# A two-layer diffusion trunk with experts: the head of the program, the norm ahead of the router and the first expert chunk in another order

## The chip, the cores and the metric

The kernel runs on one core of one Trainium2 chip. The metric is the device time of one execution in microseconds (us), lower is better; several executions are taken and their median is compared. A time below is counted from the start of the profiled span.

## The reference

Two layers work on 256 latent tokens `x` and 256 context tokens `ctx`, each 1024 wide, in float32. Each layer turns a conditioning vector into six modulation rows (shift, scale, gate, twice), for latent tokens from `c` and for context tokens from `c_ctx`. Every sub-layer is `h = x * (1 + scale) + shift; x <- LayerNorm(alpha * x + gate * sublayer(h))`. Cut to what matters:

```python
sc, scc = silu(c), silu(c_ctx)
for l in range(2):
    mod_x = sc @ w_mod[l] + b_mod[l]          # 6 rows of 1024, mod_c alike from scc
    shx1, scx1, gx1, shx2, scx2, gx2 = split(mod_x, 6)
    hx, hc = x * (1 + scx1) + shx1, ctx * (1 + scc1) + shc1
    if l == 0: yx, yc = _mixer_ab(...)        # projection, windowed + neighbourhood attention, output projection
    else:      yx, yc = _mixer_c(...)         # differential attention, latent queries only are needed
    x = _layernorm(DN_ALPHA * x + gx1 * yx, ln_g[l, 0], ln_b[l, 0])
    if l == 0:                                # dense SwiGLU on both streams, norms of ctx and x
        ...
    else:
        h = x * (1 + scx2) + shx2
        logits = h @ w_router                 # 8 experts, top 2 per token, softmax of the two
        f = sum over experts of gate[:, e] * (silu(h @ w_up_g[e]) * (h @ w_up_u[e])) @ w_down[e]
        x = _layernorm(DN_ALPHA * x + gx2 * f, ln_g[l, 1], ln_b[l, 1])
```

## The kernel before

One function, `trunk()`, writes each engine's program by hand, and engines wait for each other on semaphores only. What stands earlier in an engine's program runs earlier: no scheduler reorders it. SP issues the DMAs of all weights, in chunks of 1 MB (128 partitions x 2048 float32), into a ring `RAW` of four slots; the experts' chunks go into a ring of eight (`RAWA`, `RAWB`). A slot is loaded again when its chunk has been used.

**Precision.** Each float32 product is three matmuls (`mm3`, L762 to L764). The operands are a high part (rounded to fp32r) and a low part (the rest): ScalarE (ACT) writes the high part of a weight chunk to `WH` (L1455), VectorE (DVE) the low part to `WL` (L1881). `WH` and `WL` have two slots. The activations' parts are `HH` and `HL` (L1955, L1956); for the experts' weights they are `BH` (L1753) and `RAWAL`/`RAWBL` (L2407).

**The head.** The first eight chunks are half blocks of the modulation's weights, m0 to m7 (L662 to L665). A block is 512 of the 6 x 1024 columns, and a half block covers half the contraction. `mod_half` (L784) makes eight matmuls or four per half, ACT copies the block's rows to SBUF (`mod_row_out`, L1465), `mod_columns` (L775) turns the rows into columns, and DVE adds the bias into `MODC` (L1909): blocks 0 and 1 are the shift of sub-layer 1, blocks 2 and 3 its scale. Then come the projection's weight chunks w0, w1, ... . `h_phase(0)` transposes the tokens `X` on TensorE (PE, L815), ACT applies scale and shift on the way out of PSUM into `F` (L1481), DVE splits `F`. `project(0)` makes tiles of 128 output columns for all 512 tokens, each from eight k-steps of `mm3` (24 matmuls); w0 and w1 hold two tiles each, the first four are here called t0 to t3. The tokens are loaded on POOL's queue. POOL also builds the neighbourhood attention's bias table: rows to DRAM after all eight half blocks are used (L727), from there 16 DMAs into `BIAS` (L735), and DVE adds a mask (L1923) ahead of attention.

**Router.** After layer 1's output projection `residual(2, 1)` (L2142 to L2146) adds the gated result to `X` for the second half of the columns of token blocks 2 and 3 (the latent ones, 128 tokens each), and `norm(2)` makes the layer norm: the statistics of both blocks, one root on ACT, ACT's scaling of `X` (L1643), then on DVE a multiply by the gain and an addition of the bias from `LNR` (L2184, L2185). `h_phase(3)` transposes and modulates as above, `router()` (L1144) makes the logits, DVE and PE work out a table `TAB` of which expert takes which tokens. `experts()` gathers tokens with matmuls (`SEL`): 96 columns for the small slots, 256 for the "big" expert (L1177, L1184), copies them to `FS` and `FE` (L1735, L1741), splits `FE` into `HE` and `LE`, and starts on the experts' chunks. SP reads the experts' numbers from `TAB` into registers and issues the first eight chunks. The fourth chunk is the first one of the big expert: its parts are made after the gathered tokens' ones.

## Time and profile before

| what | us |
| --- | --- |
| median of 3 runs | 1898.12 |
| lowest and highest of them | 1897.44, 1901.23 |
| the profiled execution's own time | 1892.98 |
| its span | 1890.8 |
| PE busy in the span (93%) | 1755.0 |
| DVE busy (41%) | 782.6 |
| ACT busy (35%) | 665.5 |

The span is what the trace covers of the profiled execution; 2.2 us of its time lie around it. The trace's rows are compared with one another inside that execution, which ran 5.1 us below the median. "Busy" sums the instructions of an engine. In a timeline row, "[2.75 <-DMA ...]" says that the engine sat idle for 2.75 us before the row and what ended that. A row "x8" is eight instructions in a row and their time together.

### The profile page before, as it was taken

The numbers are of one execution on the slowest core, as the hardware profiler recorded it, in microseconds if no ns is written. First come the engines' busy times: TensorE is split into PE (matmuls) and PEld (weight loads), VectorE is DVE, ScalarE is ACT, GpSimd is POOL, SyncE is SP. The second block draws the span as 40 slices with busy tenths as digits, with TensorE's granted clock in tenths as the row PEclk, the third lists the DMA queues.
The fourth block names the chain that finished last, engine by engine and source line by source line (L and its number), as shares of the span: only waits on it lengthen the run. The fifth ranks groups of instructions, "written<-read, shape, count | busy, mean of one in ns | idle before, by whom it ended". The sixth has DMA issues, their size and how long they took to land.

```text
span 1890.8 us, 24131 instructions
## 1 busy us (share of the span) xinstructions
PE 1755.0 (93%) x9428; PEld 1216.8 (64%) x9428; DVE 782.6 (41%) x1220; ACT 665.5 (35%) x961; POOL 28.7 (2%) x52
## 2 busy tenths in 40 slices
PE   6999999899999998999768999999899999999997
PEld 3885557688888776976556556655555566565553
DVE  2334553623323255644653443333441433433344
ACT  3224554423222234324634333333334333333241
POOL 2200000000000000000000000000000000000000
PEclk9998999899999999999888999999999999999999
DMA  9734752232322544321009999999989999999986
GB/s 342 162 110 169 259 174 71 67 108 90 117 95 90 202 176 167 112 89 45 5 27 385 421 416 421 421 421 385 421 354 386 385 415 421 420 421 399 413 351 258
DMA packets 111471, 481.81 MB, mean 255 GB/s; under 512 B 8154, under 2 KB 46216, under 8 KB 62208
## 3 DMA queue, kind: packets, MB, share of 16 engines
q1 hardware_dynamic: 108192, 470.57, 63.8%
q0 software_dynamic: 3168, 9.71, 2.1%
q8 instruction: 76, 1.25, 0.3%
q14 instruction: 35, 0.29, 0.0%
HBM read 477.38 MB, written 2.87 MB: 254 GB/s over the span
## 4 chain that ended last, share of the span: by engine, by line
PE 71%; DVE 11%; DMA 8%; ACT 6%; issue 3%; SPq 0%; DVEq 0%; ACTq 0%
PE PS L762 18%; PE PS L764 17%; PE PS L763 17%; DMA RAWB<-in_w_exp_up 5%; PE PS L1254 4%; PE PS L1327 3%; PE PS L784 2%; ACT BH L1753 2%; DVE RAWAL L2407 2%; PE PS L944 1%; PE PS L1202 1%; ACT S L1509 1%; PE PS L954 1%; DMA RAW<-in_w_mod 1%; ACT S L1548 1%
## 5 line engine op out<-in xcount | busy, mean ns | idle before, releaser
L1881 DVE TENSOR_TENSOR WL<-RAW,WH 128x2048 fp32r<-128x2048 f32 (+1 forms) x63 | 142.1, 2256 | 316.1 <-ACT WH L1455 316.0
L762 PE MATMUL PS<-HH,WH 128*128 128x512 f32 (+1 forms) x584 | 225.0, 385 | 5.7 <-DVE HL L1940 4.6
L763 PE MATMUL PS<-HL,WH 128*128 128x512 f32 (+1 forms) x584 | 222.2, 380 | 0.0
L764 PE MATMUL PS<-HH,WL 128*128 128x512 f32 (+1 forms) x584 | 222.1, 380 | 0.0
L1455 ACT ACTIVATE WH<-RAW 128x2048 fp32r<-128x2048 f32 (+1 forms) x63 | 118.8, 1887 | 259.6 <-PE PS L764 228.6
L762 PE MATMUL PS<-BH,HE 128*128 128x512 f32 x448 | 182.2, 407 | 22.4 <-DVE RAWAL L2407 17.0
L2407 DVE TENSOR_TENSOR RAWBL<-RAWB,BH 128x2048 fp32r<-128x2048 f32 x42 | 96.3, 2292 | 211.0 <-ACT BH L1753 211.0
L764 PE MATMUL PS<-BH,LE 128*128 128x512 f32 x448 | 176.5, 394 | 0.0
L1753 ACT ACTIVATE BH<-RAWB 128x2048 fp32r<-128x2048 f32 x42 | 80.4, 1914 | 231.8 <-DMA RAWB<-in_w_exp_up 138.5
L2407 DVE TENSOR_TENSOR RAWAL<-RAWA,BH 128x2048 fp32r<-128x2048 f32 x42 | 96.1, 2289 | 144.8 <-ACT BH L1753 144.8
L762 PEld LDWEIGHTS PS<-BH,HE 128*128 128x128 f32 x448 | 84.7, 189 | 87.2 <-issue 33.9
L1753 ACT ACTIVATE BH<-RAWA 128x2048 fp32r<-128x2048 f32 x42 | 80.4, 1915 | 161.2 <-DMA RAWA<-in_w_exp_up 90.9
L762 PEld LDWEIGHTS PS<-HH,WH 128*128 128x128 f32 x584 | 111.5, 191 | 29.7 <-issue 5.4
L764 PEld LDWEIGHTS PS<-HH,WL 128*128 128x128 f32 x584 | 111.4, 191 | 20.7
L763 PEld LDWEIGHTS PS<-HL,WH 128*128 128x128 f32 x584 | 111.6, 191 | 20.0
L762 PE MATMUL PS<-BH,TH 128*128 128x512 f32 x224 | 93.8, 419 | 16.4 <-DVE TL L2425 16.4
L764 PEld LDWEIGHTS PS<-BH,LE 128*128 128x128 f32 x448 | 85.0, 190 | 18.7
L764 PE MATMUL PS<-BH,TL 128*128 128x512 f32 x224 | 90.3, 403 | 0.0
L763 PE MATMUL PS<-RAWAL,HE 128*128 128x512 f32 x224 | 88.8, 396 | 0.0
L763 PE MATMUL PS<-RAWBL,HE 128*128 128x512 f32 x224 | 87.8, 392 | 0.0
L762 PE MATMUL PS<-WH,HH 128*128 128x512 f32 (+1 forms) x224 | 84.4, 377 | 0.0
L763 PE MATMUL PS<-WL,HH 128*128 128x512 f32 (+1 forms) x224 | 84.0, 375 | 0.0
(313 smaller groups left out, 2723.9 us busy)
## 6 DMA issues: line engine op xcount, KB each, us to landing
RAWA<-in_w_exp_up SPq DMA_DIRECT2D x112, 1024.0 KB, 10.2
RAWB<-in_w_exp_up SPq DMA_DIRECT2D x112, 1024.0 KB, 9.8
...
```

What stands on the lines that cost most here:

```text
L762: mm(ps, ah, bh, start=start, stop=False)
L763: mm(ps, ah, bl, start=False, stop=False)
L764: return mm(ps, al, bh, start=False, stop=stop)
L784: last = mm(PS[k * LANE:(k + 1) * LANE, bank, :], ST[:, kh * 4 + k, :], w[:, k, :], start=(kh == 0), stop=(kh == 1))
L944: mm(PS[:, u % 2, 0:nk], QT[hp, qt, b * P:(b + 1) * P], KTT[hp, kt, 0:nk], start=True, stop=True).then_inc(s_sc, 1)
L954: last = nc.tensor.transpose(PS[:, 2 + n % 2, kt * P:(kt + 1) * P], S[:, i % 2, j, kt * P:(kt + 1) * P], ident)
L1254: last = mm(PS[k * LANE:(k + 1) * LANE, 4 + n % 2, :], FS[:, kh * 4 + k, j * LANE:(j + 1) * LANE], w[:, k, :], start=(kh == 0), stop=(kh = ...
L1327: last = mm(PS[k * LANE:(k + 1) * LANE, 4 + j, :], GS[:, j, st * 4 + k, :], w[:, k, :], start=(st == 0), stop=(st == NST - 1))
L1455: fn(WH[:, c % 2, 0:width(c)], raw("weight", c)[:, 0:width(c)], ACT.Copy).then_inc(s_hi, 1)
L1753: fn(BH[:, a % 2, :], expert_raw(big_at[a]), ACT.Copy).then_inc(s_bhi, 1)
L1881: v.tensor_tensor(WL[:, c % 2, 0:n], raw("weight", c)[:, 0:n], WH[:, c % 2, 0:n].bitcast(F32), ALU.subtract).then_inc(s_lo, 1)
L2407: v.tensor_tensor(expert_low(big_at[a]), expert_raw(big_at[a]), BH[:, a % 2, :].bitcast(F32), ALU.subtract).then_inc(s_blo, 1)
```

## The change

**Head.** SP loads the tokens first, then m0, m1, m2, w0, m3, w1, m4 to m7; w0 and w1 get a buffer of their own (`RAWF`). The half blocks are dealt out so that m0 to m3 give the shift and scale of the first half of the contraction (`mod_block`). PE transposes the tokens before and between the first half blocks, ACT copies them plainly to `F`, and once the modulation is there `F` is modulated in place (two of four rows of chunks by DVE, two by ACT). Then `first_half` makes k-steps 0 to 3 of t0 to t3 into four PSUM banks while m4 to m7 come in, and `project(0)` makes k-steps 4 to 7 of them. ACT's exponential for attention 1's lambda moves from the head to the start of attention 0.

**Router.** The residual and the norm go block by block. PE transposes the normalised tokens without gain and bias; these are folded into the modulation (`MODF`) beforehand. Of `F`, ACT makes rows 0 to 3 and DVE rows 4 to 7. Gain and bias are applied to `X` by POOL, beside the router, and `experts()` waits for that before it gathers. SP reads one expert's number, not all four and the number of items, ahead of its first DMA.

**First big chunk.** Its high part stands on ACT ahead of the copies of `FE`, its low part on DVE ahead of `LE`; the `FE` copies are shared between ACT and DVE.

PE at the start of the program, before: after the transposes of constants come the half blocks m0 to m3 and the columns of block 0 (`RAW` holds the half blocks, `ST` the conditioning vectors).

```order
L768 MATMUL PS<-CN,VRN 128x48
L784 MATMUL PS<-RAW,ST 32x512 [waits raw_landed0,silu_c_pad_zeroed,silu_c_ready]
L784 MATMUL PS<-RAW,ST 32x512 x3
L784 MATMUL PS<-RAW,ST 32x512 [waits raw_landed1]
L784 MATMUL PS<-RAW,ST 32x512 [waits raw_landed2]
L784 MATMUL PS<-RAW,ST 32x512 [waits raw_landed3]
L775 MATMUL PS<-CN,ROWS_AT 128x2 [waits mod_row_copied]
```

PE after the change, from the fourth half block (m3) to the third k-step of t0; L792 to L794 are `mm3`.

```order
L814 MATMUL PS<-RAW,ST 32x512 [waits raw_landed3]
L805 MATMUL PS<-CN,ROWS_PRE 128x2 [waits mod_row_copied]
L805 MATMUL PS<-CN,ROWS_PRE 128x2 x3
L792 MATMUL PS<-HH,WH 128x512 [waits h_split,weights_lo_ready]
L793 MATMUL PS<-HL,WH 128x512
L794 MATMUL PS<-HH,WL 128x512
L792 MATMUL PS<-HH,WH 128x512 [waits h_split]
L814 MATMUL PS<-RAW,ST 32x512 [waits raw_landed0,mod_row_copied]
L814 MATMUL PS<-RAW,ST 32x512 x3
L792 MATMUL PS<-HH,WH 128x512 [waits h_split]
```

The projection's matmuls now stand between the half blocks, behind a wait for the split tokens, and m4 is behind the first two of them.

DVE from the last residual block to the router, before:

```order
L2142 TENSOR_TENSOR TMP<-PS,GATE 128x512 [waits sublayer_out_in_psum,vector_chain]
L2143 SCALAR_TENSOR_TENSOR X<-X,TMP 128x512 [waits vector_chain]
L2146 BN_STATS SM<-X 128x6 [waits sublayer_out_read]
L2172 BN_AGGR SM<-SM 128x2 [waits vector_chain] x2
L2174 TENSOR_SCALAR SM<-SM 128x2 [waits vector_chain]
L2176 RECIPROCAL SM<-SM 128x2 [waits deviation_ready]
L2177 SCALAR_TENSOR_TENSOR SM<-SM 128x2 [waits vector_chain]
L2184 TENSOR_TENSOR X<-X,LNR 128x1024 [waits normalised_block,norm_rows_landed]
L2185 TENSOR_TENSOR X<-X,LNR 128x1024 [waits vector_chain]
```

The same place of DVE after the change:

```order
L2265 TENSOR_TENSOR TMP<-PS,GATE 128x512 [waits sublayer_out_in_psum]
L2301 RECIPROCAL SM<-SM 128x1 [waits deviation_ready,vector_chain]
L2302 SCALAR_TENSOR_TENSOR SM<-SM 128x1 [waits vector_chain]
L2268 SCALAR_TENSOR_TENSOR X<-X,TMP 128x512
L2271 BN_STATS SM<-X 128x6 [waits sublayer_out_read]
L2296 BN_AGGR SM<-SM 128x2 [waits vector_chain]
L2297 TENSOR_SCALAR SM<-SM 128x1 [waits vector_chain]
L2301 RECIPROCAL SM<-SM 128x1 [waits deviation_ready]
L2302 SCALAR_TENSOR_TENSOR SM<-SM 128x1 [waits vector_chain]
L2312 TENSOR_SCALAR F<-PS,SM 128x256 [waits h_transposed] x4
```

The four 128x1024 operations are off DVE, and block 2's factors stand inside block 3's residual. POOL has the four now (here those of block 2; block 3's are alike), ahead of the accumulators' zeroing:

```order
L770 DMA WR<-in_w_router 128x8x8 [waits router_pad_zeroed]
L777 ISA
L777 TENSOR_TENSOR X<-X,LNR 128x1024 [waits h_transposed,normalised_block,norm_rows_landed]
L779 TENSOR_TENSOR X<-X,LNR 128x1024 [waits last_norm_scaled]
L783 MEMSET ACC_119 128x512 [waits small_token_selection_ready]
```

So POOL reads and writes `X` while DVE and PE are at the router.

SP ahead of the first expert chunk, before (`TENSOR_LOAD` reads a number of `TAB` into a register):

```order
L648 TENSOR_LOAD TAB [waits slot_table_ready,weights_lo_ready]
L648 ISA x2
L681 TENSOR_LOAD TAB
L681 ISA x2
L691 ISA
L691 DMA RAWA<-in_w_exp_up 128x2048
```

and after the change:

```order
L707 TENSOR_LOAD TAB [waits slot_table_ready,weights_lo_ready]
L707 ISA x2
L714 ISA
L714 DMA RAWA<-in_w_exp_up 128x2048
L707 TENSOR_LOAD TAB
L707 ISA x2
```

Before, the rows of L681 stand there four times, so five numbers are read ahead of the first DMA; after, it is one, and the next is read behind the second DMA.

The diff, cut to its core:

```diff
-        for c in range(C_MOE):
...
+        for part in (("mod", 0), ("mod", 1), ("mod", 2), ("weight", 0), ("mod", 3), ("weight", 1),
+                     ("mod", 4), ("mod", 5), ("mod", 6), ("mod", 7)):
...
             loads.append(("weight", c))
...
-        pos = {("mod", m): m for m in range(2 * MOD_PRE)}
...
+        pos = {key: i for i, key in enumerate(key for key in loads if key not in early)}
...
+        def mod_block(n):
+
+            return (0, 2, 1, 3)[n] if n < MOD_PRE else n % NB_MOD
...
+            for b in range(2):
+                sp.dma_start(X[:, b, :], ctx_in[0, b * P:(b + 1) * P, :]).then_inc(s_x, 16)
+                sp.dma_start(X[:, 2 + b, :], x[0, b * P:(b + 1) * P, :]).then_inc(s_x, 16)
...
-            for c in range(2 * MOD_PRE):
-                if c >= RING:
...
-                load_mod(c)
...
             for what, c in loads:
-                before, cb = order_of[pos[what, c] - RING]
...
-                sp.wait_ge(s_lo if before == "weight" else s_modused, cb + 1)
+                if (what, c) not in early and pos[what, c] >= RING:
+                    before, cb = order_of[pos[what, c] - RING]
+                    sp.wait_ge(s_lo if before == "weight" else s_modused, cb + 1)
...
-            last_i = last_load(sp)
+            sp.wait_ge(s_tab, 1)
...
-                for n, who in enumerate((0, 1, 2, "big")):
-                    e[who] = sp.value_load(TAB[0:1, bass.ds(i + (TE + n * NI), 1)], min_val=0, max_val=NE - 1)
...
+                    if who not in e:
+                        n = 3 if who == "big" else who
+                        e[who] = sp.value_load(TAB[0:1, bass.ds(i + (TE + n * NI), 1)], min_val=0, max_val=NE - 1)
...
+            last_i = last_load(sp)
...
 
+            for b in (2, 3):
+                xb = X[:, b, :]
+                gp.wait_ge(s_lnr, 96)
+                gp.wait_ge(s_xh, ln_before[2] + b - 1)
+                gp.wait_ge(s_hps, h_before[3] + 2 * (b - 1))
+                gp.tensor_tensor(xb, xb, LNR[:, 0, :], ALU.mult).then_inc(s_gpx, 1)
+                gp.wait_ge(s_gpx, b - 1)
...
-            mod_rows(0, MOD_PRE, 2)
+            turn_tokens(range(0, 4))
+            mod_half(0, 0, 6)
+            mod_half(0, 1, 6)
+            turn_tokens(range(4, 6))
+            mod_half(1, 0, 7)
+            turn_tokens(range(6, KT))
+            mod_half(1, 1, 7)
+            mod_columns(0, 2)
+            mod_columns(1, 2).then_inc(s_modcol, 1)
+            pe.wait_ge(s_lo, 1)
+            first_half(0, 0, 0, range(0, 2))
+            pe.wait_ge(s_modrow, 1)
+            mod_half(2, 0, 6)
+            first_half(0, 0, 0, range(2, 4))
+            mod_half(2, 1, 6)
+            first_half(1, 0, 1, range(0, 4))
+            pe.wait_ge(s_modrow, 2)
+            mod_half(3, 0, 7)
+            mod_half(3, 1, 7)
+            pe.wait_ge(s_lo, 2)
+            first_half(2, 1, 0, range(0, 4))
+            mod_columns(2, 3)
+            mod_columns(3, 3).then_inc(s_modcol, 1)
+            first_half(3, 1, 1, range(0, 4))
...
+                for b in (2, 3):
+                    pe.wait_ge(s_xh, ln_before[2] + b - 1)
+                    for dt in range(KT):
+                        last = nc.tensor.transpose(PS[:, dt // 4 * 2 + b - 2, dt % 4 * P:(dt % 4 + 1) * P],
...
-                        for k in range(KT):
+                        for k in range(4 if l == 0 and t[0] < 4 else 0, KT):
...
+                for k in (0, 4, 1, 5, 2, 6, 3, 7):
+                    if k < 4:
+                        pe.wait_ge(s_hf, h_before[3] + k + 1)
+                    else:
+                        pe.wait_ge(s_hfv, k - 3)
...
+                pe.wait_ge(s_ln, ln_before[3])
...
-            for n in range(MOD_PRE):
-                mod_row_out(n, n % 2)
-            act.wait_ge(s_lam, 1)
-            fn(LT[:, 2:4], LT[:, 0:2], ACT.Exp).then_inc(s_lame, 1)
...
+            def modulate_first(half):
+
+                act.wait_ge(s_xt, KT)
+                act.wait_ge(s_modc, half + 1)
+                for dt in (4 * half + 2, 4 * half + 3):
+                    for s, lo in ((1, 0), (0, CTX)):
+                        last = fn(F[:, dt, lo:lo + 256], F[:, dt, lo:lo + 256], ACT.Identity,
+                                  bias=MODC[:, 0, dt, s:s + 1], scale=MODC[:, 0, 8 + dt, s:s + 1])
+                    last.then_inc(s_hf, 2)
...
+            tokens_out(range(0, 4))
+            mod_row_out(0, 6)
+            tokens_out(range(4, KT))
+            split(1)
+            mod_row_out(1, 7)
+            modulate_first(0)
+            split(2)
+            mod_row_out(2, 6)
+            mod_row_out(3, 7)
+            modulate_first(1)
...
+                act.wait_ge(s_hps, h_before[3] + 3)
+                for dt in range(4):
+                    fn(F[:, dt, CTX:TOK].rearrange("p (b q) -> p b q", b=2), PS[:, 0:2, dt * P:(dt + 1) * P],
+                       ACT.Identity, bias=MODF[:, 0, dt:dt + 1], scale=MODF[:, 1, dt:dt + 1]).then_inc(s_hf, 1)
...
+            def norm_router():
+
+                for i, b in enumerate(ln_blocks(2)):
+                    act.wait_ge(s_var, 8 + i + 1)
+                    fn(SQ[:, b:b + 1], SV[:, b:b + 1], ACT.Sqrt).then_inc(s_std, 1)
+                    act.wait_ge(s_rs, 8 + i + 1)
+                    fn(X[:, b, :], X[:, b, :], ACT.Identity, bias=NMR[:, b:b + 1], scale=RS[:, b:b + 1])\
                         .then_inc(s_xh, 1)
...
-            for dt in range(KT):
-                act.wait_ge(s_gat, dt // 2 * 2 + 2)
...
+            act.wait_ge(*expert_landed(big_at[0], 0))
+            fn(BH[:, 0, :], expert_raw(big_at[0]), ACT.Copy).then_inc(s_bhi, 1)
+            for kh in range(2):
+                for dt in (4 * kh, 4 * kh + 1):
+                    act.wait_ge(s_gat, 4 * kh + 2)
+                    fn(FE[:, dt, :], PS[:, dt // 2, dt % 2 * BIG:(dt % 2 + 1) * BIG], ACT.Identity,
+                       bias=MODC[:, 1, 24 + dt, 0:1], scale=MODC[:, 1, 32 + dt, 0:1]).then_inc(s_gev, 2)
+                act.wait_ge(s_fev, 2 * kh + 2)
+                gathered_hi(0, kh)
...
-                    if isinstance(i, int):
-                        big_hi(0)
...
+
+                for j in range(4):
+                    dt = 4 * half + j
+                    if j < 2:
+                        for s, lo in ((1, 0), (0, CTX)):
+                            last = v.tensor_scalar(F[:, dt, lo:lo + 256], F[:, dt, lo:lo + 256], MODC[:, 0, 8 + dt, s:s + 1],
+                                                   MODC[:, 0, dt, s:s + 1], ALU.mult, ALU.add)
+                        link(last)
+                    else:
+                        dve.wait_ge(s_hf, 4 * half + 2 * (j - 1))
+                    link(v.tensor_copy(HH[:, dt, :], F[:, dt, :]))
+                    v.tensor_tensor(HL[:, dt, :], F[:, dt, :], HH[:, dt, :].bitcast(F32),
+                                    ALU.subtract).then_inc(s_hr, 1)
...
+            split(1)
+            first_columns(0, 2)
+            dve.wait_ge(s_modc, 1)
+            dve.wait_ge(s_xt, KT)
+            first_split(0)
+            split(2)
+            first_columns(1, 3)
+            dve.wait_ge(s_modc, 2)
+            first_split(1)
...
+                if between:
+                    between()
...
+                residual_block(2, 1, 2)
+                variance(2)
+                residual_block(2, 1, 3, lambda: scale(2))
+                variance(3)
+                scale(3)
+                for dt in range(4, KT):
+                    dve.wait_ge(s_hps, h_before[3] + 4)
+                    v.tensor_scalar(F[:, dt, CTX:TOK].rearrange("p (b q) -> p b q", b=2),
+                                    PS[:, 2:4, (dt - 4) * P:(dt - 3) * P], MODF[:, 1, dt:dt + 1], MODF[:, 0, dt:dt + 1],
+                                    ALU.mult, ALU.add).then_inc(s_hfv, 1)
...
+                link(v.tensor_tensor(MODF[:, 0, :], scale, b, ALU.mult))
+                v.tensor_tensor(MODF[:, 0, :], MODF[:, 0, :], shift, ALU.add)
+                v.tensor_tensor(MODF[:, 1, :], scale, g, ALU.mult).then_inc(s_modf, 1)
...
+                for dt in (4 * kh + 2, 4 * kh + 3):
+                    dve.wait_ge(s_gat, 4 * kh + 4)
+                    v.tensor_scalar(FE[:, dt, :], PS[:, dt // 2, dt % 2 * BIG:(dt % 2 + 1) * BIG],
...
+            gathered_odd(0)
+            dve.wait_ge(s_bhi, 1)
+            v.tensor_tensor(expert_low(big_at[0]), expert_raw(big_at[0]), BH[:, 0, :].bitcast(F32), ALU.subtract)\
+                .then_inc(s_blo, 1)
+            gathered_lo(0, 0)
+            gathered_odd(1)
+            gathered_lo(0, 1)
             dve.wait_ge(s_ini, 4)
-            gathered_lo(0, 0)
-            gathered_lo(0, 1)
...
-                    if first:
-                        big_lo(0)
```

## Rows read from the trace of the kernel before

**Rows 1.** Windows view: start:end, us, busy time (instructions) of PE, PEld, DVE, ACT, POOL, granted clock, DMA share, GB/s.
```profile
18.00:22.00 4.00, 1.93 (x8) 0.20 (x8) 0.00 (x0) 0.00 (x0) 0.00 (x0) 1.00 0.96 286
...
38.00:39.00 1.00, 1.00 (x7) 1.00 (x6) 0.00 (x0) 1.00 (x1) 0.00 (x0) 0.53 1.10 349
1020.00:1030.00 10.00, 10.00 (x59) 6.54 (x58) 0.69 (x1) 3.38 (x4) 0.00 (x0) 1.00 0.92 333
1170.00:1210.00 40.00, 37.55 (x228) 23.57 (x220) 14.31 (x15) 13.03 (x18) 0.00 (x0) 1.00 1.01 421
```

**Rows 2.** Chain of waits, experts' first chunks: start, us, what the chain went through.
```profile
1048.99 9.77 DMA RAWB<-in_w_exp_up
```

**Rows 3.** Timeline of the head: start, us, engine, line, operation, out<-in, count, [idle before <-releaser].
```profile
22.77 1.93 PE L784 MATMUL PS<-RAW,ST 128*32 128x512 f32 x8 [2.75 <-DMA RAW<-in_w_mod]
...
24.64 1.87 PE L775 MATMUL PS<-CN,ROWS_AT 128*128 128x2 f32 x8
...
35.82 1.67 POOL L727 DMA_DIRECT2D bias_rows<-ZP  x1 [26.42 <-PE PS L784]
...
37.09 0.19 DVE L1909 TENSOR_TENSOR MODC<-PS,VT 128x32 f32<-128x32 f32 x1 [12.56 <-PE PS L775]
...
53.27 0.60 ACT L1499 ACTIVATE QT<-PS 128x512 f32<-128x512 f32 x1 [5.08 <-PE PS L764]
...
59.24 1.91 ACT L1455 ACTIVATE WH<-RAW 128x2048 fp32r<-128x2048 f32 x1
...
69.62 0.60 ACT L1499 ACTIVATE QT<-PS 128x512 f32<-128x512 f32 x1 [4.84 <-PE PS L764]
```

**Rows 4.** Chain of waits in attention 0: eight matmuls of half a block.
```profile
173.44 1.04 PE PS L784 x8
```

**Rows 5.** Costliest groups, DVE, shapes apart: count, busy us, mean ns of one, idle before.
```profile
L2024 DVE TENSOR_SCALAR S<-S,SM 128x256 f32<-128x256 f32 x32 | 9.9, 351 | 0.6
L1956 DVE TENSOR_TENSOR HL<-F,HH 128x512 fp32r<-128x512 f32 x8 | 5.5, 692 | 0.3
L1955 DVE CAST HH<-F 128x512 fp32r<-128x512 f32 x8 | 3.4, 420 | 0.0
```

**Rows 6.** View of one tile, BIAS: duration ns min/median/max, first and last start us.
```profile
L735 POOL DMA_DIRECT2D BIAS<-bias_rows x16: 684/724/771, 60.1 to 70.3; - x16
L1923 DVE SCALAR_TENSOR_TENSOR BIAS<-BIAS,CN x2: 2282/2286/2291, 115.7 to 118.0; 128x2048 f32<-128x2048 f32 x2
```

**Rows 7.** Timeline from the last residual block to the finished table.
```profile
967.56 0.69 DVE L2142 TENSOR_TENSOR TMP<-PS,GATE 128x512 f32<-128x512 f32 x1 [0.23 <-PE PS L764]
...
971.06 2.37 ACT L1643 ACTIVATE X<-X,SM 128x1024 f32<-128x1024 f32 x2 [0.43 <-DVE SM L2177]
972.40 1.22 DVE L2184 TENSOR_TENSOR X<-X,LNR 128x1024 f32<-128x1024 f32 x1 [1.38 <-ACT X L1643]
...
977.33 3.31 PE L815 MATMUL PS<-CN,X 128*128 128x128 f32 x16 [9.88 <-DVE X L2185]
978.12 3.75 ACT L1481 ACTIVATE F<-PS,MODC 128x256 f32<-128x256 f32 x8 [4.69 <-PE PS L815]
...
982.58 0.38 ACT L1704 ACTIVATE LSUM<-PS 128x256 f32<-128x256 f32 x1 [0.71 <-PE PS L1144]
...
989.69 0.17 DVE L2306 CAST TAB<-PS 1x36 int32<-1x36 f32 x1
```

**Rows 8.** Timeline behind the table: POOL zeroing beside a small DVE operation.
```profile
993.83 2.21 POOL L753 MEMSET ACC<- 128x512 f32 x4 [47.24 <-DVE SEL L2319]
...
994.55 0.56 DVE L2392 TENSOR_SCALAR SM<-SM 128x2 f32<-128x2 f32 x1
```

**Rows 9.** Timeline of the experts' start: SP's first DMAs, the gathers, the big expert's first matmul.
```profile
993.11 2.12 SPq L691 DMA_DIRECT2D RAWA<-in_w_exp_up  x4
...
993.87 7.00 PE L1177 MATMUL PS<-SEL,X 128*128 128x96 f32 x32 [4.39 <-issue]
...
1014.22 0.72 PE L762 MATMUL PS<-BH,HE 128*128 128x512 f32 x1 [3.71 <-DVE RAWAL L2407]
```

More of the change, by code:

```diff
@@ L335, in trunk @@
         loads = []
[L336 to L337 removed]
+        m_next = 0
+        for part in (("mod", 0), ("mod", 1), ("mod", 2), ("weight", 0), ("mod", 3), ("weight", 1),
+                     ("mod", 4), ("mod", 5), ("mod", 6), ("mod", 7)):
+            loads.append(part)
+            m_next += part[0] == "mod"
+        for c in range(2, C_MOE):
             loads.append(("weight", c))
```

195 lines of the change are left out of this document (102 added, 93 removed).

## The prediction

> **What bounds the kernel now.** First the windows view. In the experts' up phase the queue moves 421 GB/s at a share of 1.01 while PE is busy 37.55 of 40 us, and between 1020 and 1030 it moves only 333 [rows 1]. Then the chain of waits: there it goes through a wait of 9.77 us for an expert's chunk [rows 2], and pieces like it recur up to 1361. So a first expert DMA that is issued earlier moves that phase as a whole, and PE's idle time in it is no gain. Then the timelines of the two places ahead of which nothing can be prefetched into use: the head, where no projection matmul can start before all eight half blocks are in and turned [rows 3], and the stretch from the last residual block to TAB, where PE and the queue stand still behind DVE, ACT, PE and ACT in turn [rows 7]. In both the reader is to see one step after the other, so a microsecond taken out there comes out at the end.
>
> **Head.** Before, the shift and scale are ready at 37.28, tile t0 leaves at 53.27 and t3 at 69.62 [rows 3]. That is (69.62 - 53.27)/3 = 5.45 per tile of 24 matmuls, 2.73 per half tile. What counts is when t3 is done: from there on the two programs are the same.
> After: the tokens are 2 MB on either queue, so ahead of m3 only w0 is new, 1 MB. At 349 GB/s, the rate while chunks and other transfers share the queue, it costs 3.0. Ahead of m3 the queue now dips to 286 GB/s for 4 us [rows 1] which I read as the ring of four running short behind PE; w0 has a buffer of its own and keeps the queue full, which at 421 would save (1 - 286/421) x 4 = 1.3. So m3 is used from 22.77 + 3.0 - 1.3 = 24.5.
> From there, with PE at the lower clock level as in the rows at 22.77 and 24.64 (half block 1.93, columns of a block taken as 1.87): half block to 26.4, two blocks' columns to 30.2, MODC 0.19 to about 30.45 [rows 3]. DVE then makes k-step 0 from two modulations at 0.35, a cast at 0.42 and a subtraction at 0.69 [rows 5]: 32.3. Step 1 follows at 34.1; steps 2 and 3, modulated by ACT beside it, at 35.2 and 36.3. PE takes m4 and m5 between them and, with t1's half of 2.73, is at about 41.8. Then m6 and m7, 1.04 each at the upper level [rows 4], to 43.9, t2's half to 46.6, two blocks' columns to 48.6, MODC 48.85. Meanwhile t3's half runs to 51.3. DVE's second round gives steps 4 to 7 at 50.7, 52.5, 53.6 and 54.7: t0 ends about 55.4, the other three second halves at 63.6. Gain against the end of t3's matmuls (69.5): **5.9**. With every PE step at the upper level (1.04 for 1.93, columns in proportion) the same list ends at 60.0: a gain of 9.6. The rows at 22.77 and 24.64 are at the lower level in just this phase, but now transposes keep PE busier before them, so I take **7**, nearer the slow list; ends 4 and 11.
> Covers. The third chunk's split (ACT 1.91 [rows 3], DVE 2.29 with the waits between, 4.85 in all) now has only two half tiles, 5.5, to hide behind after t1: 0.6 of room; without it t4 is late by what is over. The bias table's store is issued when the last half block is used, 35.82 before [rows 3], about 44 after. Its 16 DMAs then start 8 us later than 60.1 to 70.3, and each takes up to 9.9 us to land: about 88. DVE wants the table at 115.7 [rows 6], now 108.7, which leaves 20. The exponential's table load goes to ACT's start of attention, which waits for the projection anyway: nothing.
>
> **Router.** Before: the last residual starts at 967.56, transposes at 977.33, router sums leave at 982.58 [rows 7]. After: block 2's statistics are 12 matmuls (2.7 us) ahead, so its scaling on ACT (2.37/2 = 1.19 [rows 7]) runs 968.7 to 969.9 and its eight transposes are done by 971.5. Block 3: the residual's three operations of 0.7 from 967.56, 0.4 for block 2's factors in between, the variance at 970.5, the factors 971.15, ACT 972.4, transposes (3.31/2 with the wait) 974.0. F: ACT 4 x 0.46 to 975.1, DVE 4 x 0.42 to 975.8, the last router matmuls 976.6. Gain **6.0**: four DVE operations of 1.22 [rows 7], less the hand-over.
> But POOL now runs four 128x1024 operations from about 971.7, and DVE's many small operations on the way to TAB run beside them. No row has such an operation on POOL. From below: 1.22 each, DVE's own time [rows 7]. From above: three streams at the pace of POOL's zeroing, 128x512 in 2.21/4 = 0.55 [rows 8], twice that for 1024 and three times for the streams, 3.3. I take 2.1, near the middle. They end at 980.3 (976.6 to 985). In the zeroing row, a DVE operation on 128x2 took 0.56 where 0.17 is the time of one as small [rows 7, 8], so POOL's work does hold DVE up. DVE's first cast is due at 978.4, and if it stands until POOL is through, 2.0 is lost (0 to 5.7). Net for TAB: **4.0** (0.3 to 6.7).
> The rule of the Trainium skill, page "SBUF — State Buffer", section "Who interferes with whom", is that the two engines share a port pair and that a DVE operation with two SBUF inputs or in a two-port mode waits for the whole of a GpSimd instruction. By it a small DVE operation can stand for a full POOL instruction each time; the 0.56 [rows 8] agrees. The page "GPSIMD Engine Reference", section 3.1, gives 4497 ns for a float32 add of 128x2048, an estimate of 2.25 for 1024: the sum would be 0.6 worse.
>
> **Experts' start.** TAB is written at 989.69 + 0.17 = 989.86 and SP's first DMA stands at 993.11, 3.25 later, with five numbers read in between [rows 7, 9]. One number instead of five, at 3.25/5 = 0.65 each: **2.6** earlier. The dip to 333 GB/s at 1020 to 1030, (1 - 333/421) x 10 = 2.1 [rows 1], is the queue waiting for slots whose first user is the big chunk that PE starts only at 1014.22 after 3.71 of idling behind its low part [rows 9]. With the split ahead of the copies that idle time nearly goes, and PE starts about 3.65 sooner after TAB; I take **1.5** of the 2.1. PE doesn't become the bound: 37.55 of 40. If the dip doesn't close, the term is 2.6. The copies of `FE` go from ACT alone to ACT and DVE, so HE isn't later than the low part.
>
> **Sum.** 7 + 4.0 + 2.6 + 1.5 = 15.1. The profiled execution took 1892.98, so 1877.9; the median stood 5.1 above it: **1883.0**. Low terms (4 + 0.3 + 2.6) give 1891.2, high terms (11 + 6.7 + 4.7) 1875.7.
>
> **The rivals.**
> A, as forecast: 1883.0, own range 1878 to 1888.
> B, PE at the upper clock level through the head and no hold-up by POOL: 9.6 + 6.0 + 4.1 = 19.7, 1878.4. For it: PE has transposes between the half blocks. Against: 1.93 and 1.87 in the rows.
> C, POOL's first multiply starts late: the order shows an extra instruction of POOL ahead of it, and no row tells its time. If the four of 2.1 fall wholly behind the small DVE chain's start, their 8.4 us stand in it, and 6.0 turns into -2.4: 7 - 2.4 + 4.1 = 8.7, 1889.4.
> The Trainium skill, "GPSIMD Engine Reference", section 2.1, says that the first call of a freshly loaded routine pays about 6 us; no row here shows it, and it would be this case.
> D, the bias table comes late: with its DMAs over 20 us slower than 9.9 (they are small transfers and now start beside other weight chunks), DVE's mask waits and attention with it; 27 us slower eats the head's 7, then 1890 to 1896.
> E, slower: the gather waits for POOL. It stands at TAB + 4.2 (993.87 [rows 9]), new at about 989.9, and now waits for the second addition. From 971.7 that is 18.2 us, reached at 4.5 us for each of the four; beyond that each us costs four: (18.2 + 15.1)/4 = 8.3 each and all is gone, and at 9.3 each the kernel is 3.9 slower: 1902. Against: zeroing's pace gives 3.3.
> F, the change does not do what it says: the half tiles run but t3 ends no sooner because the split of the third chunk is late. That is the low end of the head, 4, and inside A's range.
>
> **How the numbers follow.** 0.2% is 3.8 us, about what a measurement of this kernel can tell from no change: faster means below 1894.3, slower above 1901.9. Chances: A 0.57, B 0.20, C 0.13, D 0.06, E 0.04. A, B and C are faster; D is taken as within 0.2%; E is slower. So faster 0.90, same 0.06, slower 0.04. The range must hold 8 in 10: from 1874, the high terms and a little for a run-to-run offset other than 5.1, to 1892, which takes in the low terms; D and E stay out.
>
> **What would show it.** Head: the last copy of t3 at 62 to 64 instead of 69.62; m3's half block near 24.5, and 1.93 or 1.04 beside it telling A from B; the third chunk's WH right behind t1. Router: LSUM's copy about 976.6 less the head's shift, four POOL operations of about 2.1, and the small DVE rows with or without gaps beside them. Experts: the first DMA 0.65 after TAB, the big expert's first matmul some 20.8 after TAB, no dip in the window behind. Wrong is the prediction if m3 lands past 27, if a POOL operation takes over 4.5 us, if PE's wait for BIAS appears in attention 0, or if the experts' up phase shows PE and not the queue as what ends the waits.

## The result

| | before | after |
| --- | --- | --- |
| median, us | 1898.12 (7 runs) | 1885.07 (7 runs, 1881.5 to 1890.0) |
| ratio, 95% interval | | 0.9932 (0.9909 to 0.9955) |
| profiled execution, us | 1892.98 | 1890.0 |
| span | 1890.8 | 1887.8 |

The kernel became 13 us faster; the interval reaches from 8.5 to 17.3 us. Forecast were 1883.0 and 15.1 us. Of the seven runs of the kernel before six lie between 1893.84 and 1904.55; the seventh took 2225.34 and does not enter the ratio.

The two profiled executions differ by only 3 us: before's lies 5.1 below its median, after's 4.9 above its own. So the profiles are read stage by stage, and not by their ends. The top of the page of after:

```profile
span 1887.8 us, 24162 instructions
## 1 busy us (share of the span) xinstructions
PE 1754.6 (93%) x9428; PEld 1216.9 (64%) x9428; DVE 786.9 (42%) x1239; ACT 663.3 (35%) x954; POOL 35.9 (2%) x52
```

PE does the same work in the same time, and POOL has 7 us more. The change is in the order of the work, so the timelines are what to read.

**Head**, timeline of after, beside [rows 3]. Columns as there.

```profile
26.70 1.76 PE L814 MATMUL PS<-RAW,ST 128*32 128x512 f32 x8 [3.49 <-DMA RAW<-in_w_mod]
...
32.00 0.17 DVE L2010 TENSOR_TENSOR MODC<-PS,VT 128x16 f32<-128x16 f32 x1 [3.60 <-PE PS L805]
...
34.28 0.77 PE L792 MATMUL PS<-HH,WH 128*128 128x512 f32 x1 [2.32 <-DVE HL L2025]
...
45.52 1.92 PE L814 MATMUL PS<-RAW,ST 128*32 128x512 f32 x16
...
59.30 0.60 ACT L1599 ACTIVATE QT<-PS 128x512 f32<-128x512 f32 x1 [4.80 <-PE PS L794]
...
64.55 2.29 DVE L1981 TENSOR_TENSOR WL<-RAW,WH 128x2048 fp32r<-128x2048 f32 x1 [5.72 <-ACT WH L1526]
...
67.48 0.60 ACT L1599 ACTIVATE QT<-PS 128x512 f32<-128x512 f32 x1 [2.12 <-PE PS L794]
```

The projection starts at 34.28 and t0 to t3 leave in steps of 2.7, but t3 leaves at 67.48 against 69.62 before: 2.1 gained, not 7, and outside the 62 to 64 that the prediction gave as its sign. PE waits 3.49 for m3 and uses it at 26.70, not 24.5; past 27 the prediction would have called itself wrong.

**Router**, timeline of after, beside [rows 7].

```profile
975.50 0.69 DVE L2265 TENSOR_TENSOR TMP<-PS,GATE 128x512 f32<-128x512 f32 x1
...
979.20 2.34 POOL L777 TENSOR_TENSOR X<-X,LNR 128x1024 f32<-128x1024 f32 x1 [25.75 <-PE PS L882]
...
986.35 2.34 POOL L779 TENSOR_TENSOR X<-X,LNR 128x1024 f32<-128x1024 f32 x1
...
987.61 1.11 DVE L2406 CAST SM<-IDX 128x16 f32<-128x16 uint32 x1
...
994.11 0.17 DVE L2446 CAST TAB<-PS 1x36 int32<-1x36 f32 x1
...
995.33 3.13 SPq L714 DMA_DIRECT2D RAWA<-in_w_exp_up  x4
...
998.30 6.09 PE L1248 MATMUL PS<-SEL,X 128*128 128x96 f32 x32 [4.41 <-DVE SEL L2459]
...
1013.97 0.50 PE L792 MATMUL PS<-BH,HE 128*128 128x512 f32 x1
```

From the last residual block to the written TAB it is 994.28 - 975.50 = 18.8, before 22.3. POOL's operations take 2.34. A cast of DVE that takes 0.17 otherwise takes 1.11, and ends at 988.72, when POOL's last one has ended (988.69). SP's first DMA stands 1.05 behind TAB instead of 3.25, the big expert's first matmul 19.7 behind it instead of 24.4. The queue's dip of [rows 1] is gone, in the last line of this windows view of after (the first two are needed further down):

```profile
2.00:6.00 4.00, 0.25 (x1) 0.18 (x1) 0.00 (x0) 0.01 (x1) 4.00 (x9) 1.00 0.96 191
6.00:10.00 4.00, 0.47 (x2) 0.18 (x1) 1.01 (x5) 0.32 (x2) 1.34 (x3) 1.00 0.78 297
...
1020.00:1030.00 10.00, 10.00 (x66) 6.03 (x68) 2.46 (x2) 3.21 (x5) 0.00 (x0) 1.00 1.01 422
```

The first two of these windows before the change:

```profile
2.00:6.00 4.00, 0.17 (x1) 0.17 (x1) 0.00 (x0) 0.01 (x1) 4.00 (x9) 1.00 0.82 278
6.00:10.00 4.00, 0.55 (x2) 0.19 (x2) 0.33 (x1) 0.31 (x2) 3.40 (x7) 1.00 1.02 422
```

**Where this execution loses it again.** Although t3 is 2.1 us earlier, the last residual block starts 7.9 later (975.50 against 967.56). Some 8 of these 10 us are lost in attention 0: the last low part of a weight chunk ahead of it starts at 143.57 (before: 145.71), ACT's first write of `GATE` behind it at 307.4 (before: 301.4). The windows view of that stretch, first before, then after:

```profile
155.00:310.00 155.00, 142.00 (x1065) 83.10 (x1066) 82.07 (x380) 83.87 (x237) 1.13 (x2) 0.94 0.53 184
```

```profile
155.00:310.00 155.00, 141.31 (x1034) 80.75 (x1033) 79.52 (x377) 81.33 (x234) 1.13 (x2) 0.90 0.51 180
```

The granted clock is 0.94 in the one and 0.90 in the other: after's execution spent more of attention 0 at the lower of PE's two levels. The longest waits there are for the same operations in both.

### The profile page after: what moved, and what is told of

Same layout as the page of the kernel before. It is cut to its first block, busy times and chain, and to the rows that moved or that the text cites. A ratio compares the mean times of both kernels' runs of the same rounds, so it can differ in the third digit from the quotient of the medians.

```text
span 1887.8 us, 24162 instructions
## 1 busy us (share of the span) xinstructions
PE 1754.6 (93%) x9428; PEld 1216.9 (64%) x9428; DVE 786.9 (42%) x1239; ACT 663.3 (35%) x954; POOL 35.9 (2%) x52
## 4 chain that ended last, share of the span: by engine, by line
PE 73%; DVE 10%; DMA 8%; ACT 6%; issue 3%; SPq 0%; DVEq 0%; ACTq 0%
PE PS L792 18%; PE PS L793 17%; PE PS L794 17%; DMA RAWB<-in_w_exp_up 5%; PE PS L1326 4%; PE PS L1399 3%; PE PS L814 2%; DMA RAWA<-in_w_exp_down 2%; ACT BH L1855 2%; PE PS L1012 2%; PE PS L1273 1%; DVE RAWAL L2560 1%; ACT S L1609 1%; PE PS L1022 1%; DMA RAW<-in_w_mod 1%
## 5 line engine op out<-in xcount | busy, mean ns | idle before, releaser
L1981 DVE TENSOR_TENSOR WL<-RAW,WH 128x2048 fp32r<-128x2048 f32 (+1 forms) x61 | 137.6, 2256 | 310.7 <-ACT WH L1526 310.6
L792 PE MATMUL PS<-HH,WH 128*128 128x512 f32 (+1 forms) x584 | 226.2, 387 | 8.2 <-DVE HL L2068 4.6
L794 PE MATMUL PS<-HH,WL 128*128 128x512 f32 (+1 forms) x584 | 222.8, 382 | 0.0
L792 PE MATMUL PS<-BH,HE 128*128 128x512 f32 x448 | 181.6, 405 | 19.3 <-DVE RAWAL L2560 12.9
L794 PE MATMUL PS<-BH,LE 128*128 128x512 f32 x448 | 176.1, 393 | 0.0
L792 PEld LDWEIGHTS PS<-BH,HE 128*128 128x128 f32 x448 | 84.5, 189 | 84.0 <-issue 30.2
L792 PEld LDWEIGHTS PS<-HH,WH 128*128 128x128 f32 x584 | 111.9, 192 | 35.0 <-issue 11.1
L794 PEld LDWEIGHTS PS<-HH,WL 128*128 128x128 f32 x584 | 111.8, 191 | 20.8
L792 PE MATMUL PS<-BH,TH 128*128 128x512 f32 x224 | 91.9, 410 | 19.3 <-DVE TL L2578 19.2
L794 PEld LDWEIGHTS PS<-BH,LE 128*128 128x128 f32 x448 | 84.5, 189 | 18.5
L794 PE MATMUL PS<-BH,TL 128*128 128x512 f32 x224 | 88.5, 395 | 0.0
L792 PE MATMUL PS<-WH,HH 128*128 128x512 f32 (+1 forms) x224 | 85.0, 379 | 0.0
```

What stands on the lines that cost most here:

```text
L792: mm(ps, ah, bh, start=start, stop=False)
L794: return mm(ps, al, bh, start=False, stop=stop)
L1981: v.tensor_tensor(WL[:, c % 2, 0:n], raw("weight", c)[:, 0:n], WH[:, c % 2, 0:n].bitcast(F32), ALU.subtract).then_inc(s_lo, 1)
```

## The experiments

With a profile of every kernel the stages can be set beside each other. All figures are differences of starts in the timelines, in us. "t3" is ACT's copy of t3 (from the span's start), "middle" from there to DVE's last residual block of layer 1, "to TAB" from there to TAB written, "DMA" and "big" from TAB to SP's first expert DMA and to the big expert's first matmul, "ninth" from TAB to the ninth low part of a big chunk on DVE, up to which the experts' start shows; from there to the 29th all kernels take 198.0 to 198.6.

| kernel | t3 | middle | to TAB | DMA | big | ninth | ratio to before (interval) |
| --- | --- | --- | --- | --- | --- | --- | --- |
| before | 69.6 | 897.9 | 22.3 | 3.2 | 24.4 | 103.3 | 1 |
| after | 67.5 | 908.0 | 18.8 | 1.0 | 19.7 | 99.0 | 0.9932 (0.9909, 0.9955) |
| after_again | 65.5 | 900.1 | 18.6 | 1.0 | 19.9 | 98.9 | 0.9928 (0.9907, 0.9949) |
| head_only | 65.9 | 907.3 | 22.2 | 3.2 | 23.4 | 103.4 | 0.9981 (0.9966, 0.9995) |
| no_head | 69.2 | 906.6 | 18.6 | 1.0 | 19.9 | 99.0 | 0.9949 (0.9934, 0.9965) |
| split_late | 67.4 | 904.1 | 18.6 | 1.0 | 23.7 | 104.0 | 0.9952 (0.9935, 0.997) |
| five_loads | 67.2 | 904.0 | 18.6 | 3.2 | 21.3 | 101.4 | 0.993 (0.9904, 0.9957) |
| x_on_pool | 67.3 | 900.4 | 18.6 | 1.0 | 19.9 | 98.9 | 0.993 (0.9909, 0.9951) |
| w0_behind | 66.2 | 904.0 | 18.6 | 1.0 | 19.9 | 98.9 | 0.9916 (0.9892, 0.994) |
| pool_late | 66.1 | 900.3 | 17.6 | 1.0 | 26.8 | 105.3 | 0.9941 (0.9921, 0.9961) |
| w0_mid | 64.1 | 904.2 | 18.6 | 1.0 | 19.9 | 99.1 | 0.9911 (0.9888, 0.9933) |
| gain_split | 65.9 | 906.7 | 17.6 | 1.0 | 20.3 | 99.0 | 0.9919 (0.9897, 0.9941) |
| head_warm | 63.1 | 912.0 | 18.6 | 1.0 | 19.9 | 99.0 | 0.9921 (0.9891, 0.995) |
| best | 64.0 | 903.9 | 17.6 | 1.0 | 20.4 | 99.0 | 0.9894 (0.9874, 0.9915) |

"To TAB" and "ninth" repeat within 0.2 wherever the code is the same. "Middle" is nearly the same code in all of them (a few small operations differ between before and after) and differs by 14 us, by 12 among the kernels with after's code there (900.1 to 912.0). From the ninth low part to the end of the span it is 793.4 to 800.0, again with nearly the same code. Each kernel has one profile, and "t3" itself is 65.5 to 67.5 with the same head. An edit of 1 to 4 us is therefore read in its stage, and the ratios confirm only sums.

**The changed kernel again**, with no edit.

> The changed kernel once more, for a second profile and its time beside the parts. Theory 1 (the change is worth the sum of four stage gains read from the first profile of it: head 2.1 us, norm and router 3.5, first expert DMA 2.2, queue's dip 2.1, about 10 in all; the rest of the measured 13 and the 8 us that its profile lost in attention 0 are how often PE fell to its lower clock level in that execution): the stage gains repeat within 0.5 us each, t3's copy stands at about 67.5, and the time lost in attention 0 does not repeat, or elsewhere. Theory 2 (the later phase of the weights' queue or the shifted program itself costs 8 us in attention 0): the same stretch is 8 us longer than before again.

Behind the middle the stages repeat within 0.2. The head doesn't: t3 stands at 65.51 and not at 67.5. m3 is used at 26.27 (26.70 in after), but its half block takes 1.07 instead of 1.76, and the granted clock from 37 to 41 is 0.90 instead of 0.55. The middle takes 900.1 instead of 908.0. In the windows view of this second execution the clock in attention 0 is above before's:

```profile
155.00:310.00 155.00, 142.85 (x1077) 85.98 (x1077) 80.31 (x371) 84.93 (x236) 1.13 (x2) 0.96 0.54 191
```

Theory 2 falls: the 8 us belong to one execution and not to the change.

**The head alone.** The kernel before with the head's part of the change (`first_half`, `turn_tokens`, the new order of loads); router and experts as before.

> The kernel before with the head's part of the change alone. Theory 1 (head worth 2.1 us in the profile: the tokens on SP's queue ahead of the half blocks delay m3 to 26.7, and PE starts the projection at 34.3 on the lower clock level): t3's copy at about 67.5 against 69.62, ratio to before 0.999, 1896. Theory 2 (the forecast's 7 us, the first profile was unlucky): t3's copy at 62 to 65, ratio 0.996, 1891.

t3 at 65.9, between the two theories' values, and 0.9981: 3.6 us, interval 0.9 to 6.5. The forecast's 7 is outside. The measured 3.6 fits the stage, 69.4 (the mean of the two profiles with the old head) less 65.9.

**All but the head.** The changed kernel with the kernel before's order of loads and `h_phase(0)`.

> The changed kernel with the head of the kernel before; router, experts' first DMA and first big chunk as changed. Theory 1: the gains behind the head are about 8 us, ratio 0.9955 to 0.996, 1890. Theory 2 (head worth 7, the rest 6 of the 13): ratio 0.997, 1892. In the profile, the stretch from the last residual block to TAB is 3.5 us shorter and SP's first DMA stands about 1.05 after TAB in either.

0.9949, 9.7 us (6.6 to 12.5). Head and rest add up: 3.6 + 9.7 = 13.3 against 13.0 and 13.7 for both together. The stages say 3.7 + 4.4 = 8.1 for the rest, inside the interval; theory 1.

**The big chunk's split late again.** The edit also gives all copies of `FE` back to ACT, so it tests this part of the change as a whole and not the split by itself.

```diff
-            act.wait_ge(*expert_landed(big_at[0], 0))
-            fn(BH[:, 0, :], expert_raw(big_at[0]), ACT.Copy).then_inc(s_bhi, 1)
...
                 def up():
+                    if isinstance(i, int):
+                        big_hi(0)
```

> The changed kernel with the first big expert chunk split behind the gathered tokens' copies, all of them on ACT, as before. Theory 1 (the queue's dip of 2.1 us at the experts' start closes because the big chunk is ready sooner): the window of 10 us about 27 to 37 us behind TAB shows some 333 GB/s again, and the time is 2 us above the changed kernel's. Rival (the dip closed because the first DMAs are issued sooner and the eight slots fill later against PE): the window stays at 420 GB/s and the time is the same within 0.5 us.

The window, in this kernel:

```profile
1020.00:1030.00 10.00, 10.00 (x59) 6.54 (x58) 1.43 (x2) 3.42 (x4) 0.00 (x0) 1.00 0.65 234
```

The dip is back and deeper than either side expected, 234 GB/s where before had 333, and the ninth low part comes 5.0 later. The first DMA is still 2.2 earlier than before, and this buys nothing: 104.0 against before's 103.3. With the slots filled sooner the queue only waits longer for the big chunk's first use: from 30 to 35 us behind TAB it moves 102 GB/s, before 313. The rival falls. In time it is 0.9952 against 0.9928, 4.6 us, near the stage's 5.0, though the two intervals overlap.

**All five numbers read first, split early.**

```diff
-            sp.wait_ge(s_tab, 1)
+            last_i = last_load(sp)
...
+                for n, who in enumerate((0, 1, 2, "big")):
+                    e[who] = sp.value_load(TAB[0:1, bass.ds(i + (TE + n * NI), 1)], min_val=0, max_val=NE - 1)
                 for q, (who, what, st, h) in enumerate(order):
-                    if who not in e:
...
```

> The changed kernel with SP reading all five numbers ahead of its first expert DMA, as before; the big chunk's split early, as changed. Theory 1 (the queue sets the experts' up phase, each us of its start comes through): the first DMA at TAB plus 3.25, the big expert's ninth low part at 101 behind TAB against 99.0, and 2 us more in time. Rival (the big chunk's first use sets it, which needs the gather and not the queue): the ninth low part stays at 99 to 99.5 behind TAB. The version with the split late had 104.0 with the early DMA, more than the 103.3 of the kernel before, so the two are not plainly additive.

The ninth low part is at 101.4, 2.4 later than in the changed kernel, with the first DMA 2.2 later: theory 1. The time (0.993) can't tell 2 us apart. Together with split_late: the split (with the shared copies) alone is worth 103.3 - 101.4 = 1.9, the early DMA alone 103.3 - 104.0 = -0.7, both 4.3. The split gains by itself; the early DMA gains only on top of it, and then 2.4. Why it costs 0.7 without it was not tested.

**The tokens on POOL's queue.**

```diff
 # the program of gpsimd
+            for b in range(2):
+                gp.dma_start(X[:, b, :], ctx_in[0, b * P:(b + 1) * P, :]).then_inc(s_x, 16)
+                gp.dma_start(X[:, 2 + b, :], x[0, b * P:(b + 1) * P, :]).then_inc(s_x, 16)
```

> The changed kernel with the tokens on POOL's queue again, as before; all else of the head as changed. In four profiles with the tokens at the head of SP's queue, m3 is used at 26.3 to 26.7 and the queue moves 191 and 297 GB/s in the windows 2 to 6 and 6 to 10, where before moved 278 and 422. Theory 1 (SP's order costs these 2 us): m3 at 24.3 to 24.8, t3's copy at 64 to 65.5, 2 us less than the changed kernel's 65.7 to 67.7. Rival (w0's small rows and not the tokens take that time): m3 stays at 26 or later.

m3 is late, as the rival forecast, but w0 is not the reason. Timeline and windows of this kernel:

```profile
18.74 3.64 PE L825 MATMUL PS<-CN,X 128*128 128x128 f32 x16 [12.17 <-DMA X<-in_x]
...
27.40 1.06 PE L814 MATMUL PS<-RAW,ST 128*32 128x512 f32 x8
```

```profile
2.00:6.00 4.00, 0.16 (x1) 0.16 (x1) 0.00 (x0) 0.01 (x1) 4.00 (x9) 1.00 0.83 268
6.00:10.00 4.00, 0.56 (x2) 0.20 (x2) 1.01 (x5) 0.31 (x2) 3.43 (x7) 1.00 1.02 419
18.00:22.00 4.00, 3.26 (x16) 3.27 (x16) 0.00 (x0) 1.63 (x3) 0.00 (x0) 1.00 0.80 237
```

The queue is faster from 2 to 10 with w0 in the same place, so the slow start goes with the tokens at the head of SP's queue, as theory 1 has it. But the tokens now land only at 18.7, and PE's transposes stand ahead of m0 in its program. PE comes to m0 at 22.31 (17.03 in after) and to m3 at 27.40, without a wait for m3's data: what is late here is PE, not the queue. The ring runs dry behind it (237 GB/s from 18 to 22), which concerns m4. So this run doesn't show what the queue's slow start costs; that is worked out below, from the next run. t3 is where it was, at 67.3.

**w0 behind m3.**

```diff
-        for part in (("mod", 0), ("mod", 1), ("mod", 2), ("weight", 0), ("mod", 3), ("weight", 1),
+        for part in (("mod", 0), ("mod", 1), ("mod", 2), ("mod", 3), ("weight", 0), ("weight", 1),
...
-            split(1)
             mod_row_out(1, 7)
+            split(1)
```

> The changed kernel with w0 loaded behind m3 and its high part made behind block 1's rows. Theory (m3 is what the first k-step waits for, w0's split has 2 us to spare): m3 at 24, MODC at about 29.5 but w0's low part at about 31, so the first k-step gains 1 us and t3's copy about as much. Rival (w0's split then ends last): nothing gained, t3's copy at 66 to 67.5.

```profile
23.74 1.06 PE L814 MATMUL PS<-RAW,ST 128*32 128x512 f32 x8 [0.46 <-DMA RAW<-in_w_mod]
...
28.76 2.29 DVE L1981 TENSOR_TENSOR WL<-RAWF,WH 128x2048 fp32r<-128x2048 f32 x1 [20.87 <-ACT WH L1526]
...
30.97 0.17 DVE L2010 TENSOR_TENSOR MODC<-PS,VT 128x16 f32<-128x16 f32 x1
```

m3 is used 3.0 earlier than in after. MODC comes at 30.97, behind w0's low part, and t3 at 66.2, against a mean of 66.5: the rival. The next edit takes that away:

```diff
+                    if mid and j == 0:
+                        mid()
-            split(1)
             first_columns(0, 2)
...
-            first_split(0)
+            first_split(0, lambda: split(1))
```

> The kernel with w0 behind m3, and on DVE the first columns and the first k-step's own operations ahead of w0's low part. With w0 only moved behind m3, m3 was used at 23.7 but MODC came at 30.97, behind w0's low part on DVE. Theory: MODC at 26.9, w0's low part at 31.1 ends last, the first k-step starts at 31.2 instead of 33.2 and t3's copy stands at 64 to 65. Rival (from there on PE is held by the half blocks and by the second half of the tokens' split, not by its own start): t3's copy stays at 66.

The timeline of this kernel:

```profile
23.42 1.07 PE L814 MATMUL PS<-RAW,ST 128*32 128x512 f32 x8 [0.42 <-DMA RAW<-in_w_mod]
...
26.48 0.17 DVE L2010 TENSOR_TENSOR MODC<-PS,VT 128x16 f32<-128x16 f32 x1 [18.63 <-PE PS L805]
...
28.53 2.28 DVE L1981 TENSOR_TENSOR WL<-RAWF,WH 128x2048 fp32r<-128x2048 f32 x1
```

m3 3.3 us earlier than in after, and t3 at 64.1, against 65.5 to 67.5 with the order of the changed kernel. The rival falls: the first k-step starts at 30.87, and t3 follows it by 33.3, much as in after (33.2), so t3 moves with PE's start.

**PE kept busy ahead of m3.**

```diff
+            def keep_busy(n):
+                for _ in range(n):
+                    nc.tensor.transpose(PS[:, 3, 0:P], X[:, 0, 0:P], ident)
...
             turn_tokens(range(6, KT))
+            keep_busy(20)
             mod_half(1, 1, 7)
             mod_columns(0, 2)
             mod_columns(1, 2).then_inc(s_modcol, 1)
+            keep_busy(12)
```

> The changed kernel with 32 transposes whose results nobody reads, 20 in PE's wait for m3 and 12 in its wait for the first k-step. Theory (PE's idling ahead of m3 is followed by the lower level from 27 to 41, and that is the difference between the forecast's two lists): the granted clock stays at the upper level, the half block m3 takes 1.06 and the first k-steps' matmuls 0.4 instead of 0.63, and t3's copy stands at 63.5 to 65 each time. Rival (the lower level comes whatever PE does there): the same durations as in the changed kernel and t3's copy at 66 to 68.

Windows view from 27 to 41, first of after, then of this kernel:

```profile
27.00:41.00 14.00, 11.56 (x42) 6.61 (x35) 9.45 (x15) 4.47 (x6) 0.00 (x0) 0.51 0.85 337
```

```profile
27.00:41.00 14.00, 12.24 (x76) 7.59 (x68) 9.44 (x15) 5.07 (x7) 0.00 (x0) 1.00 1.04 400
```

The granted clock is 1.00 instead of 0.51, which is 2.4 against 1.2 GHz, 76 matmuls go through instead of 42, and t3 stands at 63.1. m3 is used at 26.60, as in after, so the gain is the clock's. The lower level in the head follows on PE's idling there and costs 2.4 to 4.4 us. The time (0.9921) doesn't show it: this execution's middle took 912.0, the longest of all, with a clock of 0.90 from 155 to 310. Whether an earlier or warmer head is paid for there, or this is one more draw, stays open: over all kernels the middle is 898 to 912 with no plain relation to t3.

**POOL's work behind TAB.**

```diff
+            gp.wait_ge(s_tab, 1)
             for b in (2, 3):
                 xb = X[:, b, :]
```

> The changed kernel with POOL's four operations on the tokens started only when TAB is ready. Theory (they hold DVE's cast up by 0.94 us, 1.11 against 0.17, and the gather waits for the last of them): the cast takes 0.17, the residual to TAB stretch is 17.7 instead of 18.7; the gather starts at TAB + 9.5 instead of + 4.0, and the time is 4 to 5 us above the changed kernel's. Rival (the cast is slow for another reason): 1.11 again. If the gather's delay is absorbed by waits for the queue, the time rises by less than 2.

DVE's row, and the gather's:

```profile
978.52 0.18 DVE L2407 CAST SM<-IDX 128x16 f32<-128x16 uint32 x1
```

```profile
993.94 7.12 PE L1249 MATMUL PS<-SEL,X 128*128 128x96 f32 x32 [10.37 <-DVE SEL L2460]
```

The cast takes 0.18 and the stretch 17.6: POOL costs the router 1.0. The gather comes at TAB + 10.0 instead of 4.0, and all of it arrives at the ninth low part (105.3 against 99.0). By the stages the time should rise by 5.3 (1.0 less, 6.3 more), as the expectation's 4 to 5; the ratio rises by 1.7 to 2.5 us against the changed kernel's two. The intervals overlap, so the time doesn't decide this.

**Block 2's gain and bias on DVE.**

```diff
-            for b in (2, 3):
+            for b in (3,):
...
                 scale(3)
+                dve.wait_ge(s_lnr, 96)
+                dve.wait_ge(s_hps, h_before[3] + 2)
+                link(v.tensor_tensor(X[:, 2, :], X[:, 2, :], LNR[:, 0, :], ALU.mult))
+                v.tensor_tensor(X[:, 2, :], X[:, 2, :], LNR[:, 1, :], ALU.add).then_inc(s_ln, 1)
```

> The changed kernel with block 2's gain and bias on DVE, in the 3.3 us in which it waits for the transposes, and only block 3's on POOL. Theory (DVE's cast stands until POOL's last operation has ended): POOL is through before the cast is due, the cast takes 0.17 instead of 1.1, residual to TAB takes 17.7 instead of 18.6, with no later gather: 0.9 us faster, which the time alone can hardly show. Rival: DVE's two operations take longer beside POOL or push its four F rows back, and the stretch stays at 18.6.

Timeline of this kernel, DVE and then POOL:

```profile
976.55 1.22 DVE L2312 TENSOR_TENSOR X<-X,LNR 128x1024 f32<-128x1024 f32 x1 [0.50 <-PE PS L882]
...
984.70 0.17 DVE L2410 CAST SM<-IDX 128x16 f32<-128x16 uint32 x1
```

```profile
981.97 2.34 POOL L779 TENSOR_TENSOR X<-X,LNR 128x1024 f32<-128x1024 f32 x1
```

POOL ends at 984.31, the cast starts at 984.70 and isn't held up, and the stretch is 17.6. "Ninth" is counted from the earlier TAB and stays 99.0, so the gain of 1.0 comes through to the experts. The time (0.9919) can't show 1 us.

**Both of the better versions together.** The edits of w0_mid and gain_split.

> The changes of w0_mid and gain_split together. If both do what they should, 2 to 3 us below the changed kernel: 0.9915 to the kernel before, against 0.993.

t3 64.0, to TAB 17.6, ninth 99.0; median 1879.84, ratio 0.9894 (0.9874 to 0.9915). Its median is 19.6 us under that of the kernel before in the same runs (1899.43). By the ratios it is some 7 us under the changed kernel, where 2 to 3 were expected; the stages account for 3.5 (66.5 to 64.0, and 1.0), and the rest isn't explained. Its interval ends below the changed kernel's 0.9928 and 0.9932, though theirs reach down to 0.9907.

## Why the prediction was right, and where not

The time came true (1883.0 forecast, 1885.07 measured), and with it case A's range. Of the sum of 15.1 the stages show 10.9, inside the measured 8.5 to 17.3: too much by 4.2, nearly all in one term. The medians gained 2 to 3 us more than the stages show (13.0 and 13.7 in the two series, 13.3 from the parts); no run shows where. They bring the measured time nearer to the forecast than its terms deserve, and that is luck.

- **Head, 7 forecast, 2.9 measured** (t3 at 65.5 to 67.5 in seven profiles with this head, 66.5 in the mean, against 69.4 in the two with the old one). The direction and the order of steps held. Against after's own profile the 4.9 missing divide so. The step "m3 is used from 22.77 + 3.0 - 1.3 = 24.5" failed: 26.70, 2.2 late. The price for w0, 3.0, held: m3 is used at 26.6 in the mean of the seven and at 23.6 in the mean of the three profiles with w0 behind it. The dip closed too: 424 GB/s from 18 to 22 in w0_behind, 286 before. So 21.5 was due without w0, and 2.1 are missing there. What the step left out is that with the tokens at the head of SP's queue it moves 191 and 297 GB/s from 2 to 10 where before it moved 278 and 422, which is (87 + 125) x 4 / 421 = 2.0 us. That is worked out and fits; no run tests it by itself. MODC then came 5.3 behind m3 and not 5.95, the first k-step 2.3 behind MODC and not 1.85. From there to t3 it is 33.2 instead of 31.3. The list has the first half tiles at the upper level, but up to 41 they ran at the lower one (a matmul 0.63 to 0.80, behind it 0.40); in head_warm, at the upper level throughout, it is 31.2. The last 1.1 was mine: the list at the lower level gave 5.9, and 7 was taken in the hope of the upper one. What the level is worth was right: 3.7 between the two lists, 3.4 between the mean and head_warm. One reading under it is open: the list takes before's half block of 1.93 for the lower level, and in after that duration does go with a granted clock of 0.50, but before's own windows give 1.00 from 22 to 30.
- **Router, 4.0 forecast, 3.7 measured.** 6.0 less a hold-up of 2.0 was forecast; measured are 4.7 (pool_late, 22.3 - 17.6) less 1.0. Both terms were too large, and the errors nearly cancel. The reason given for 6.0, four DVE operations of 1.22 less the hand-over, makes 4.9 at most; the rest came from the list of steps. That the cast stands until POOL is through is what happened. POOL ended only 1.1 after the cast was due, not 2.0, since the logits too were later: their sums left 10.3 behind the last residual block's start (985.76) and not 9.0. POOL's operation was 2.34, not 2.1. The term's bounds were loose: POOL's end between 976.6 and 985 gives a hold-up of 0 to 6.6, not 5.7, and a net of -0.6 to 6.0, not 0.3 to 6.7. The rule of the Trainium skill, "SBUF — State Buffer", "Who interferes with whom", held: DVE's wait ends with POOL's instruction, 988.72 against 988.69. It was this one operation only; DVE's four rows of `F` out of PSUM took 0.54 each beside POOL and 0.54 without it (pool_late). The 2.25 estimated from the Trainium skill, "GPSIMD Engine Reference", section 3.1, was nearer than the 2.1 taken from rows.
- **Experts, 4.1 forecast, 4.3 measured**, with a wrong reason in it. The first DMA came 2.2 earlier (2.6 forecast). "If the dip doesn't close, the term is 2.6" failed: in split_late it doesn't close and the term is -0.7. Only in the order split first (1.9, 1.5 forecast), DMA on top (2.4, 2.6 forecast) do the two add as forecast. The queue's start gains nothing by itself; the first use of the slot it then needs has to move with it.
- **Covers.** The third chunk's low part was done at 66.84, and t4's first matmul stands at 67.96: it hid, with 1.1 of room where 0.6 was forecast. The bias table's DMAs went from 67.8 to 77.9, and DVE took the table at 113.6, before 115.7: no wait.
- **The rivals.** B: half of it, the upper level in the head, exists (head_warm) but not in this kernel. C fell: POOL's first operation started 0.19 behind PE's last transpose of block 2, and took what the others took, 2.34. D and E fell with the rows above; pool_late shows E's mechanism to be real: a gather late by 6.0 comes through with 6.3.
- **The offset.** To add the 5.1 between before's profile and its median was right; after's profile by itself, at 1890.0, would have said that 3 us were gained.
